# Squares summed on VectorE, waits moved inside the down products, staggered first tiles and four column strips in the feed-forward stages of a two-block network

## The reference, cut to what matters

```python
def rms_norm(x, gain):
    return x * lax.rsqrt(jnp.mean(x * x, axis=-1, keepdims=True) + RMS_EPS) * gain
def swiglu(h, w_gate, w_up, w_down):          # D_FF = 2816
    return (jax.nn.silu(h @ w_gate) * (h @ w_up)) @ w_down
for layer in range(DEPTH):                    # DEPTH = 2
    f = swiglu(rms_norm(h, g[0]), ...);  h = h + 0.5 * rms_norm(f, g[1])
    mix = pool_mixer(...) if layer == 0 else dilated_mixer(...)
    h = h + rms_norm(mix, g[3])
    f = swiglu(rms_norm(h, g[4]), ...);  h = h + 0.5 * rms_norm(f, g[5])
# pool_mixer: u = h @ w_in; four groups of 256 channels: moving mean minus u, @ w_group; then @ w_out
# second block, per layer: shift, scale, gate = split(silu(c) @ w_ada + b_ada, 3), for c and for c_ctx
```

## Time and profile before

| what | value |
|---|---|
| median of 3 runs | 4001.14 us (3999.13 to 4002.23) |
| the profiled execution, its own time | 4002.51 us |
| its span in the profile | 4000.7 us |
| PE busy | 3443.0 us, 86% of the span, 20464 matmuls |
| DVE, ACT, POOL busy | 40%, 29%, 30% |
| mean granted clock of TensorE | 0.924 of full speed |
| feed-forward, pool and dilated stages | from 25 us to about 2385 us of the span |

### The profile page before, as it was taken

The page is one execution under the profiler, slowest core; times in us unless marked ns, Lnnn a source line. Parts: engine busy times, 40 slices in busy tenths (PEclk is TensorE's granted clock), DMA queues, the critical chain, the costliest instruction groups (busy, mean ns, idle before and its releaser), DMA issues. The chain is left out here.

```text
span 4000.7 us, 52988 instructions
## 1 busy us (share of the span) xinstructions
PE 3443.0 (86%) x20464; PEld 2525.6 (63%) x20464; DVE 1611.0 (40%) x2625; ACT 1152.1 (29%) x1959; POOL 1202.2 (30%) x998
## 2 busy tenths in 40 slices
PE   6999788999799988998899978787988867778787
PEld 5777566677577675776667757564655655455554
DVE  3233434233333235443424236543553256544533
ACT  3222223122321122111322123433433223434332
POOL 2444343333233342221234334210330123113211
PEclk9999999999899999999999989878979988889879
DMA  3222121333223321111232321000001111000011
GB/s 121 90 89 89 59 79 63 116 98 117 77 94 116 120 84 53 58 53 48 71 110 97 121 85 58 22 12 21 28 17 53 43 48 38 22 17 33 22 43 42
DMA packets 73773, 263.02 MB, mean 66 GB/s; under 512 B 7792, under 2 KB 9072, under 8 KB 73200
## 3 DMA queue, kind: packets, MB, share of 16 engines
q1 hardware_dynamic: 67104, 242.25, 18.0%
q10 hardware_dynamic: 6480, 18.11, 1.2%
HBM read 250.89 MB, written 7.34 MB: 65 GB/s over the span
## 5 line engine op out<-in xcount | busy, mean ns | idle before, releaser
L847 POOL TENSOR_TENSOR wl<-raw,wh 128x1024 fp32r<-128x1024 f32 x320 | 779.5, 2436 | 1480.5 <-ACT wh L956 1027.5
L1291 PE MATMUL ps<-xh,wh 128*128 128x512 f32 x2400 | 920.5, 408 | 132.0 <-POOL wl L835 39.6
L1291 PE MATMUL ps<-xl,wh 128*128 128x512 f32 x2400 | 871.9, 388 | 0.0
L1291 PE MATMUL ps<-xh,wl 128*128 128x512 f32 x2400 | 868.4, 386 | 0.0
L1291 PEld LDWEIGHTS ps<-xh,wh 128*128 128x128 f32 x2400 | 448.7, 198 | 316.6 <-issue 175.9
L956 ACT ACTIVATE wh<-raw 128x1024 fp32r<-128x1024 f32 x248 | 262.8, 1060 | 1116.1 <-PE ps L1291 1063.3
L1291 PE MATMUL ps<-ah,wh 128*128 128x512 f32 x1104 | 459.1, 423 | 78.5 <-DVE al L1970 60.1
L835 POOL TENSOR_TENSOR wl<-raw,wh 128x1024 fp32r<-128x1024 f32 x90 | 219.5, 2439 | 979.0 <-ACT wh L934 979.0
L1291 PEld LDWEIGHTS ps<-xl,wh 128*128 128x128 f32 x2400 | 448.3, 198 | 94.1 <-issue 11.4
L1291 PEld LDWEIGHTS ps<-xh,wl 128*128 128x128 f32 x2400 | 445.4, 197 | 89.9
L1291 PE MATMUL ps<-al,wh 128*128 128x512 f32 x1104 | 430.0, 397 | 0.0
(11 more groups left out here) (333 smaller groups left out, 3787.7 us busy)
## 6 DMA issues: line engine op xcount, KB each, us to landing
raw<-wts_dram SPq DMA_DIRECT2D x458, 512.0 KB, 3.4
spilled_dram<-hc ACTq DMA_DIRECT2D x1, 3072.0 KB, 9.1
hc<-spilled_dram ACTq DMA_DIRECT2D x1, 3072.0 KB, 12.4
hc<-x_dram ACTq DMA_DIRECT2D x8, 256.0 KB, 9.0
spilled_dram<-hc ACTq DMA_DIRECT2D x1, 2048.0 KB, 7.2
hc<-spilled_dram ACTq DMA_DIRECT2D x1, 2048.0 KB, 9.1
out_dram<-hc SPq DMA_DIRECT2D x8, 256.0 KB, 2.0
hc<-ctx_dram ACTq DMA_DIRECT2D x1, 1024.0 KB, 12.0
```

Of the source, the lines that this page charges most:

```text
L847: pool.tensor_tensor(wl[:, n % SPLIT, :], raw[:, LOADED[n] % RAW, :], wh[:, n % SPLIT, :].bitcast(F32), ALU.subtract).then_inc(lo_done, 1)
L1291: ins = pe.matmul(out_, w[:, s, k * P:(k + 1) * P], x_(k, at), start=first, stop=last)
```

## The change

The diff does six things.

1. *Squares.* At the end of a stage ACT squares chunk m right behind its conversion in tile m (`f_square`); DVE adds the squares of chunks 0 to 6 into one tile `sq_sum` (`add_square`), and PE makes two ones-products after the last tile (`f_norm`) in place of eight. The pool and dilated stages do the same.
2. *Waits.* After a part's gate and up tiles PE waits for all but the last `al`; the last is waited for at the last step of k of the first down tile.
3. *High part of the product.* `hi` is no longer copied from `tt`: DVE makes the product twice, once into `ah` and once into `tt`.
4. *First tiles.* Tile 1 lags tile 0 by three steps of k, and ACT converts tile 2 before it makes `rs` (`h_rstd`).
5. *Conditioning.* The two products of 512 columns become four of 256 columns, each into its own strip of 32 partitions of bank 6; `ada_rows` keeps all 128 partitions, and `turn_ada` selects the rows by a constant `sel`.
6. *Pool.* Both groups use banks 4 to 7, the second takes its blocks in the order 2, 3, 0, 1 with a wait for each half, and the first `w_out` tile takes its steps of k in the order in which the groups make them, with a wait for each.

```diff
+        sq_sum = sil[:, 0, :]
@@ ACT
+            def f_square(m):
+                n = c.take("sq")
+                if m > 2:
+                    act.wait_ge(sq_used, n - 2)
+                act.activation(sq[:, n % 2, :] if m else sq_sum, fo[:, m, :], ACT.Square).then_inc(sq_ready, 1)
...
-                for part in FF_PARTS:
+                for number, part in enumerate(FF_PARTS):
...
+                    first = 0 if number else 4
+                    for j in range(first):
+                        n = tile()
+                        if j == 0:
+                            h_rstd("ffn", layer, i)
+                        silu(0, n, j)
...
                 for m in range(KC):
-                    tile()
-                    if m:
-                        act.wait_ge(taken, c.at("tile") - 1 + 4)
-                        square(fo[:, m - 1, :])
...
+                    n = tile()
+                    act.wait_ge(taken, n + 5)
+                    f_square(m)
+                f_rstd()
@@ PE, down_and_ada
                         for k in range(part):
+                            if j == 0 and k == part - 1:
+                                pe.wait_ge(a_ready, last_part)
                             ins = mm3([ps[:, n % 4, 0:SEQ]], n % SPLIT, k, a_hi, a_lo, [0], k == 0, k == part - 1)
...
-                        for k in range(2):
-                            ins = pe.matmul(ps[0:2, 6, :], col("cc", 2 * (2 * j + k), 2), raw[:, at % RAW, k * FOUR:(k + 1) * FOUR],
-                                            start=j == 0 and k == 0, stop=j == 3 and k == 1)
+                        for lane in range(4):
+                            k, half = divmod(lane, 2)
+                            w = raw[:, at % RAW, lane * FOUR // 2:(lane + 1) * FOUR // 2]
+                            ins = pe.matmul(ps[32 * lane:32 * lane + 2, 6, 0:FOUR // 2], col("cc", 2 * (2 * j + k), 2), w,
+                                            start=j == 0, stop=j == 3, skip_group_check=True)
@@ PE
+            def f_norm():
+                n = c.take("sq", KC)
+                c.take("norm")
+                pe.wait_ge(sq_used, n + KC - 2)
+                norm_sum(sq_sum, True, False)
+                pe.wait_ge(sq_ready, n + KC)
+                norm_sum(sq[:, (n + KC - 1) % 2, :], False, True)
...
+                for k in range(KC + lag):
+                    if k < KC:
+                        pe.wait_ge(x_ready, x0 + k + 1)
+                        part(0, k)
+                        if with_squares:
+                            add_squares(k)
+                    if k >= lag:
+                        part(1, k - lag)
@@ PE, ffn
-                    wait_a(part)
+                    wait_a(part - 1)
+                    last_part = c.take("a") + 1
...
-                    if m:
-                        add_squares(m - 1)
-                add_squares(KC - 1)
+                f_norm()
@@ PE, pool
                     if g0 == 0:
-                        settle_but_this(n)
-                    pe.wait_ge(a_ready, a0 + c.take("pool group", 4) + 4)
-                    for b in range(4):
+                        pe.wait_ge(x_ready, x0 + 4)
+                    for b in group_blocks(g0):
                         g, m = g0 + b // 2, b % 2
+                        if m == 0:
+                            pe.wait_ge(a_ready, a0 + POOL_READY[g])
...
-                wait_x()
-                settle()
-                chunks(KC, KC, a_hi, a_lo)
-                norm()
...
+                    for number, k in enumerate(order):
+                        if m == 0:
+                            pe.wait_ge(x_ready, x0 + number + 1)
@@ DVE
+            def add_square(m):
+                n = c.take("sq")
+                if 0 < m < KC - 1:
+                    dve.wait_ge(sq_ready, n + 1)
+                    dve.tensor_tensor(sq_sum, sq_sum, sq[:, n % 2, :], ALU.add).then_inc(sq_used, 1)
+                    dve.wait_ge(sq_used, n)
...
+                            dve.tensor_tensor(hi, tt[:, j, :], sil[:, j, :], ALU.mult).then_inc(dve_own, 1)
                             dve.tensor_tensor(tt[:, j, :], tt[:, j, :], sil[:, j, :], ALU.mult).then_inc(dve_own, 1)
-                            dve.wait_ge(dve_own, it * 4 + (o0 + 2 * j + 1))
-                            dve.tensor_copy(hi, tt[:, j, :]).then_inc(dve_own, 1)
```

More of the change, by code:

```diff
@@ L1041, in pool @@
                     else:
-                        for b in range(4):
-                            act.activation(ahk(2 * m + b), ps[:, group_bank(m, b), :], ACT.Copy, scale=col("pscale", 2 * m + b)).then_inc(part_hi, 1)
-                tiles_loop(KC)
-                f_squares()
-                c.take("h", KC)
+                        for b in group_blocks(m):
+                            act.activation(ahk(2 * m + b), ps[:, 4 + b, :], ACT.Copy, scale=col("pscale", 2 * m + b)).then_inc(part_hi, 1)
+                for m in range(KC):
+                    n = tile()
+                    act.wait_ge(taken, n + 5)
+                    f_square(m)
+                f_rstd()
             def keep():
@@ L1351, in turn_ada @@
                 for m in range(16):
-                    ins = pe.matmul(ps[:, 7, 2 * m:2 * m + 2], ada_rows[:, m * P:(m + 1) * P], const("ident", 2)[0:2, :], start=True, stop=True)
+                    group, half, part = m // 4, m // 2 % 2, m % 2
+                    rows = ada_rows[:, (2 * group + part) * P:(2 * group + part + 1) * P]
+                    ins = pe.matmul(ps[:, 7, 2 * m:2 * m + 2], rows, const("sel")[:, 2 * half:2 * half + 2], start=True, stop=True)
                 give(ins, p2d, "p2d")
@@ L1358, in _, with norm_sum @@
             a_lo = lambda k, at: alk(k)
+            def norm_sum(src, start, stop):
+                pe.matmul(ps[:, 4 + (c.at("norm") - 1) % 2, :], ones, src, start=start, stop=stop).then_inc(sq_used, 1)
             def add_squares(k):
@@ L1364, in add_squares @@
                 pe.wait_ge(sq_ready, n + 1)
-                pe.matmul(ps[:, 4 + (c.at("norm") - 1) % 2, :], ones, sq[:, n % 2, :],
-                          start=k == 0, stop=k == KC - 1).then_inc(sq_used, 1)
-            def norm():
-                for k in range(KC):
-                    add_squares(k)
+                norm_sum(sq[:, n % 2, :], k == 0, k == KC - 1)
+            def f_norm():
[5 more added lines that the diff above has]
+                norm_sum(sq[:, (n + KC - 1) % 2, :], False, True)
             def wait_x():
@@ L1425, in pool @@
                 first_two_chunks()
[L1426 to L1429 removed]
+                a0, x0 = c.take("a", KC), c.take("x", KC)
+                for what, g0 in POOL_TILES[2:]:
                     n = tile()
@@ L1444, in pool @@
                             for w, x_, first, last in ((wh, a_hi, k == 0, False), (wh, a_lo, False, False), (wl, a_hi, False, k == 1)):
-                                ins = pe.matmul(ps[:, group_bank(g0, b), :], w[:, n % SPLIT, blk * P:(blk + 1) * P], x_(2 * g + k, 0), start=first, stop=last)
+                                ins = pe.matmul(ps[:, 4 + b, :], w[:, n % SPLIT, blk * P:(blk + 1) * P], x_(2 * g + k, 0), start=first, stop=last)
                     ins.then_inc(tile_done, 1)
-                c.take("a", KC)
-                wait_x()
-                settle()
-                chunks(KC, KC, a_hi, a_lo)
-                norm()
-            def settle_but_this(n):
-                pe.wait_ge(taken, n + 4)
+                order = [2 * g0 + b for what, g0 in POOL_TILES if what == "group" for b in group_blocks(g0)]
+                for m in range(KC):
+                    n = tile()
+                    pe.wait_ge(taken, n + 1)
+                    for number, k in enumerate(order):
+                        if m == 0:
+                            pe.wait_ge(x_ready, x0 + number + 1)
+                        ins = mm3([ps[:, n % 4, :]], n % SPLIT, k, a_hi, a_lo, [0], number == 0, number == KC - 1)
+                    ins.then_inc(tile_done, 1)
+                f_norm()
             def dilated():
@@ L2020, in pool @@
                     dve.tensor_tensor(t[:, 0:PAD], t[:, 0:PAD], pads[:, 0, PAD:2 * PAD], ALU.subtract).then_inc(part_ready, 1)
-                down_loop(True)
+                for m in range(KC):
+                    if m:
+                        add_square(m - 1)
+                    n = tile()
+                    took(dve.tensor_copy(fo[:, m, :], ps[:, n % 4, :]), n)
+                add_square(KC - 1)
                 add_f(norm_gain(0, 3), "ffn", 0, 1)
```

108 lines of the change are left out of this document (54 added, 54 removed).

## The result

The changed kernel takes 3740.39 us (median of 4 runs, 3737.53 to 3743.98), the kernel before 4001.68 in the same measurement (4 runs, 3999.13 to 4002.74): ratio 0.9348, 95% interval 0.9332 to 0.9365. That is faster by 261 us. Forecast were a gain of 273, 12 us too much, and with it 3728; 3740 lies within the forecast's own range of 3712 to 3745.

The account below looks back on a forecast made before the run. PE, busy 86% of the span, was taken as the bound, with gains only from its gaps and removed instructions. 75 + 81 + 29 + 2 + 61 + 20 + 5 = 273 us gave 3728 against the median; own range 3712 to 3745.

Parts of the forecast that it names:

- step 3: Feed-forward starts: no idle ahead of tile 2 in three stages, gain 29 us, and 2 more in stage (1, 0).
- Step 2: Feed-forward tails: tiles 4.1 us apart instead of 6.92, seven times in each of four stages; gain 81 us.
- Step 1: PE's 12 waits for a part's last `al`: 60.1 us shrink to 0.3 or 1.7 us each; gain 75 us.
- the upper end: At the `al` waits: DVE's second product stands behind POOL, ending 0.3 to 0.6 us later than the copy.
- the clock term: Slow matmuls behind each of 12 `al` waits: 2.0 us lost per wait to the low clock.
- Step 4: Conditioning: four products of 256 columns run abreast in strips, gaining 1.28 us for each of 48 pieces; 61 us.
- Step 5: Pool and dilated stages: earlier start, less idle and shorter tail; gain 20 us in pool, 5 in dilated.
- Strips run four abreast: Conditioning; the rival denied it: two abreast gives 3748, one after the other 3789; chance 0.27 together, 0.19 for two.
- new pacer: Rival in tails, pool's chain and starts: conversion, POOL or DVE's additions set a slower pace, 3750 to 3775; chance 0.15.
- The second product isn't held: Rival at the `al` waits: POOL doesn't hold DVE's second product, 9 us less, 3719; no chance given.
- the rival of the clock: Rival for the changed stages: granted clock falls when PE works almost without rest; 4050 at 0.85; chance 0.02.

Follow-up runs that it names:

- wait_undone: Changed kernel, but PE waits for all `al` ahead of the down tiles again; 3814.58 us, ratio 0.9535 to the kernel before.
- the three runs: Conditioning products in one strip (3798.51 us) or two strips (3765.19 us), each against the changed kernel, and the changed kernel itself with four strips (3740.39 us).
- tables_late: Changed kernel, but stage (1, 0)'s DVE table work and ACT's two sines moved between the first part and its down tiles; 3726.42 us, ratio 0.9313.
- The two runs of the starts: Changed kernel with one half of the feed-forward start edit undone in each: no lag (3750.38 us), or `rs` made ahead of the conversion (3749.59 us).
- start_no_lag: Changed kernel, but without the three-step lag of tile 1 in the feed-forward stages, early conversion kept; 3750.38 us, ratio 0.9377.
- start_rs_first: Changed kernel, but ACT makes `rs` ahead of converting tile 2 again in the feed-forward stages, lag kept; 3749.59 us, ratio 0.9375.

## Why the prediction was right, step by step

What each term came to, from the rows before and after, with what an experiment gave for it:

| step | forecast | by the traces | experiment |
|---|---|---|---|
| 1. waits for `al` | 75 | 70.5 | 76.0 - 5.5 |
| 2. tails | 81 | 71.3 | 72.9 |
| 3. starts | 31 | 27 | - |
| 4. conditioning | 61 | 61 | 62.1 |
| 5. pool, dilated | 25 | 31.2 | - |
| sum | 273 | 261.0 | - |

The column of the traces adds up to 261.0 because step 3 is what is left when the others are taken off. In row 1 both figures use the 1.8 us of wait_undone. No run undid the edits to pool and dilated.

**Step 2 is the one that was most off**, in size: "Both leave the loop, seven times in each of four stages." The gap of 2.83 occurs six times, since the first ones-product stood behind tile 1, and the seventh product was already in the 3.65 us at the end. 6 x 2.83 + 0.86 = 17.8 for a stage (49.15 - 31.32), 71.3 for four. What the step said of the pace (4.1, with 0.5 us to spare for the weights, POOL first) held: 4.08, and POOL's subtraction ends 0.55 us before the tile (904.40, 904.95).

**Step 1.** The mechanism held and the upper end was the right one to take. The remainder was 11.3 instead of 9.2 (0.48 and 1.83 to 1.89 for 0.3 and 1.7), and the clock term 1.8 instead of 2.0 a wait (the granted clock in the ten us behind each wait of the kernel before gives 1.9). The 5.5 are idle that wait_undone has on top of the 60.1 before, since `al` comes later with the second product than with the copy. That this product costs something the prediction saw (0.3 to 0.6 later); that the old copy is the better form (by 8.9 us), it didn't draw out.

**Step 3.** No idle is left in three stages, as forecast, and 6.81 in (1, 0), where some 9 were. The 27 are the remainder of the four stages' gains, 8.5, 8.9, 3.0 and 6.8 in order, so they hold the clock's variation. The 0.9 us for an earlier end of tile 1 did not come: from the stage's first matmul until the two tiles and their ones-products are done it is 21.1 us in (0, 1), before (606.1 to 627.19) and after (539.6 to 560.7). What is left in (1, 0) was put down to ACT's table of sines; the runs say that the sines wait for DVE's own table work, that moving them alone takes 1.75 us off, and that moving both takes all of it.

**Step 4** is right, in size and cause: four strips are abreast, and the constant of 0.33 us for a piece stayed. The Trainium skill, "TensorEngine Tiling (Array Packing)", Key Properties, says that different tiles can multiply in parallel; the three runs agree, at 1.71, 0.85 and 0.43 us of columns.

**Step 5.** Pool gained 22.5 (156.1 to 133.7) where 19.9 were forecast. By parts: the second group starts 5.1 us sooner in the stage (2.4 forecast), 8.1 are gained from there to the first output tile (8.4), 2.7 from there to the last conversion (2.7), and 6.6 from that to L974 (6.4). So the miss lies in what comes ahead of the second group. Dilated gained 8.7 where 5 were forecast: 2.6 in the idles of its start and 2.2 from the last conversion to L974, as the step said; the rest may be the clock, since this stage varies by 5 us without an edit.

That the sum came within 12 us is in part luck: steps 1 to 3 promised 18 us too much, and step 5 some 6 too little.

**The rivals.** Strips run four abreast (step 4). No new pacer came: tiles of the tail are at 4.08. A busy stretch keeps its clock: from the start of (0, 1) to its end (394 us, PE busy in 388.6) it is granted 0.99. "The second product isn't held" is out for the change as made, and true once its input lies in PSUM. In the rival of the clock a figure is off: if 0.88 costs 273 us, 0.85 costs some 350 and gives about 4080, not 4050; nothing rests on it.

## What to carry to other kernels

Count how often a stall occurs in the timeline (first and last event of the loop), not from the loop's bounds: that alone was 10 us too many. If VectorE and GpSimd work in turns, look at where the operands lie before looking at what the operation is; one input in an unused bank of PSUM took the hold away. If a wait is laid to one engine, ask what that engine itself waits for: the sines stood 3.39 us for VectorE, and moving them alone took 1.75 of 6.81 us off. And when work moves in time, look at what now runs beside it: the table work fell beside GpSimd's subtraction and lost 2.2 us. Put such side work where buffers give slack, here four banks ahead of down tiles.

## What the runs showed of the hardware that was not expected

A short wait inside a dense stream of matmuls costs more than itself even when the clock stays: 0.77 us for an idle of 0.48 and 2.18 for one of 1.89, at a granted clock of 1.00. The extra is 0.29 both times.

Operations of VectorE with one input, in SBUF, are held beside GpSimd's subtraction too: in tables_late a TENSOR_SCALAR that takes 0.43 us elsewhere takes 2.59 at 1043.18. Silu's product with one input in SBUF and one in PSUM (0.69) is not.

Gaps of 2 us may also bring the low clock. The two runs of the starts have six of them. Behind two, at 47.93 in start_no_lag and at 1764.38 in start_rs_first, the ten us that follow have 0.83; behind the other four they have 1.00. What tells them apart no run shows.

An unedited stage with equal waits varies by up to 5 us from kernel to kernel (dilated: 397.6 to 402.9), and the mixers by 17 (1592 to 1609), so a difference of a few us in the whole time tells nothing of an edit. The length of the edited stages tells more; the mark still holds what the dilated stage varies by.
